# Input projections of u and v by seven half-size products instead of eight

## The reference

```python
h = rms_norm(x, g_mix[l])
z = h @ w_in[l]                       # 512 x 1024 by 1024 x 4800
u, v, q_lat, kv_lat, k_rope, gate_a, gate_b = jnp.split(z, offs, axis=-1)
y_a = spatial_gating(gelu(u), gelu(v), ...)      # layer norm of gelu(v), mixing of rows, times gelu(u)
y_b = mla_attention(q_lat, kv_lat, k_rope, ...)
merged = sigmoid(gate_a) * y_a + sigmoid(gate_b) * y_b
x = x + merged @ w_o[l]
x = x + moe(rms_norm(x, g_ffn[l]), ...)          # 64 experts, top 8
x = x + sigmoid(rms_norm(x, g_ple_in[l]) @ w_ple_gate[l]) * rms_norm(p[l] @ w_ple_proj[l], g_ple_out[l])
```

## Time and profile before

| | us |
|---|---|
| median of 3 runs (1110.62 to 1113.02) | 1111.32 |
| the profiled execution, whole | 1110.49 |
| its span in the trace | 1108.7 |
| TensorE busy | 1092.9 (99% of the span) |
| VectorE, ScalarE, GpSimd busy | 861.2, 787.0, 423.6 |
| chunks 2 to 9, by TensorE | 44.7 to 219.0 |

### The profile page before, as it was taken

One profiled execution on the slowest core, in us unless ns is written; L12 is line 12 of the kernel. 1 busy time (PEld: TensorE's weight loads), 2 busy tenths in 40 slices (PEclk: granted clock), 3 DMA queues, 4 the chain that ended last, 5 costly groups with the idle time before them and its releaser, 6 DMA issues.

```text
span 1108.7 us, 17836 instructions
## 1 busy us (share of the span) xinstructions
PE 1092.9 (99%) x5488; PEld 914.7 (83%) x5488; DVE 861.2 (78%) x1239; ACT 787.0 (71%) x1270; POOL 423.6 (38%) x477
## 2 busy tenths in 40 slices
PE   7999999999999999999999999999999999999998
PEld 7988888878778888888888888888888888888787
DVE  4535532278765468999999999999999999999865
ACT  6644433357654343888888898889888988888772
POOL 1120000015276003355556555555655555555400
PEclk9999999999999999999999999999999999999999
DMA  7422422112402259999999999999999999999632
GB/s 251 153 76 76 142 85 76 29 57 71 158 1 71 101 225 381 356 377 382 394 393 388 391 393 388 391 391 393 395 396 396 396 394 393 392 393 359 192 151 76
DMA packets 72130, 291.60 MB, mean 263 GB/s; under 512 B 15187, under 2 KB 20598, under 8 KB 47126
## 3 DMA queue, kind: packets, MB, share of 16 engines
q1 hardware_dynamic: 52672, 254.13, 57.3%
q0 software_dynamic: 18768, 34.79, 12.5%
q10 hardware_dynamic: 646, 2.12, 0.5%
HBM read 284.61 MB, written 42.07 MB: 295 GB/s over the span
## 4 chain that ended last, share of the span: by engine, by line
PE 93%; DVE 3%; ACT 2%; POOL 1%; issue 1%; DMA 0%; ACTq 0%; POOLq 0%; DVEq 0%
PE bank L2065 11%; PE bank L2067 11%; PE bank L2066 11%; PE bank L1752 7%; PE bank L1789 6%; PE bank L1793 6%; PE bank L1790 6%; PE bank L2093 5%; PE bank L2091 5%; PE bank L2092 5%; PE bank L2030 5%; PE bank L1743 2%; PE bank L1944 1%; PE bank L2163 1%; PE bank L2165 1%; PE bank L2164 1%
## 5 line engine op out<-in xcount | busy, mean ns | idle before, releaser
L1624 DVE TENSOR_TENSOR arena_r<-arena,win_r 128x1024 fp32r<-128x1024 f32 x252 | 292.0, 1221 | 21.9 <-ACT win_r L1082 19.1
L1082 ACT ACTIVATE win_r<-arena 128x1024 fp32r<-128x1024 f32 x252 | 246.5, 1069 | 0.5 <-DMA resid<-in_w_exp_up 0.5
L2065 PE MATMUL bank<-win_r,work_r 128*128 128x512 f32 x512 | 206.5, 403 | 0.6 <-issue 0.6
L2066 PE MATMUL bank<-win_r,x_low_r 128*128 128x512 f32 x512 | 199.5, 390 | 0.0
L2067 PE MATMUL bank<-arena_r,work_r 128*128 128x512 f32 x504 | 197.4, 392 | 0.0
L1604 DVE TENSOR_TENSOR arena_r<-arena,hT_r 128x1024 fp32r<-128x1024 f32 x128 | 150.5, 1217 | 0.5 <-ACT hT_r L1090 0.5
L733 POOL DMA_INDIRECT moe_sum<-ya,sidx x64 | 111.5, 1743 | 102.7 <-ACT ya L1118 86.0
L1789 PE MATMUL bank<-arena_r,hT_r 128*128 128x512 f32 (+2 forms) x320 | 121.9, 381 | 2.2 <-DVE win_r L1222 2.1
L1790 PE MATMUL bank<-arena_r 128*128 128x512 f32 (+2 forms) x320 | 121.1, 378 | 0.0
L1793 PE MATMUL bank<-win_r,hT_r 128*128 128x512 f32 (+2 forms) x320 | 121.0, 378 | 0.0
L2067 PEld LDWEIGHTS bank<-arena_r,work_r 128*128 128x128 f32 x504 | 94.6, 188 | 21.7
(11 more groups left out here) (321 smaller groups left out, 2213.4 us busy)
## 6 DMA issues: line engine op xcount, KB each, us to landing
arena<-in_w_exp_down SPq DMA_DIRECT2D x64, 1024.0 KB
arena<-in_w_exp_gate SPq DMA_DIRECT2D x63, 1024.0 KB
arena<-in_w_exp_up SPq DMA_DIRECT2D x63, 1024.0 KB
win<-in_w_in SPq DMA_DIRECT2D x8, 2048.0 KB, 7.8
win<-in_w_o SPq DMA_DIRECT2D x2, 2048.0 KB, 7.9
arena<-in_w_ple_gate SPq DMA_DIRECT2D x2, 2048.0 KB, 13.7
arena<-moe_sum SPq DMA_DIRECT2D x7, 512.0 KB, 7.0
win<-in_mla_w_qb SPq DMA_DIRECT2D x4, 576.0 KB, 4.0
```

The lines of the kernel that those rows point to most:

```text
L1082: act.activation(gu_hi[n % 2][:, :, cols], raw[:, :, cols], ACT.Copy).then_inc(gu_hi_r, 1)
L1624: dve.tensor_tensor(low_[:, :, cols], raw[:, :, cols], gu_hi[n % 2][:, :, cols].bitcast(F32), ALU.subtract).then_inc(gu_lo_r, 1)
L2065: pe.matmul(b_, x_hi[:, k, :], w_hi, start=(k == 0), stop=False)
L2066: pe.matmul(b_, x_lo[:, k, :], w_hi, start=False, stop=False)
```

## The change

Chunks 2 to 5 (v and u) are replaced by two **pairs** `p` = 0 (v) and 1 (u). In a pair the rows (512), the inner dimension (1024) and the columns (1024) are each cut in two, and the product is made with seven products of halves in place of eight (Strassen's method in Winograd's form). One product is 2 row tiles by 4 slices by 3 matmuls of 128x512, and they run in the order `11, T1, T2, 21, 22, T3, T4`. Four products take sums of rows (`S1` to `S4`), four take sums of weight quarters (`T1` to `T4`).

- **Rows.** VectorE makes S1 to S4 from `hT_hi` and `hT_lo` (`rows_1` to `rows_4`), once for both pairs; they are split in high and low parts. `rows_1` stands ahead of the split of chunk 1, the others behind it.
- **Weights.** The sums are made by DMA: SyncE loads a quarter, and GpSimd issues a DMA that adds another quarter on top (`add_weights`, `accum_op=ADD`). `T2` adds to what `T1` left, once VectorE has made `T1`'s low part; `T4` adds to `T2`. `T1(1)` below is T1 of pair 1. Each quarter is 128 x 4 x 512 values, 1 MB. Landings are counted on two semaphores.
- **Results.** `add_products` combines PSUM banks and SBUF on VectorE (14 instructions of 128x512 per pair), ScalarE copies the first product out and applies gelu in SBUF.
- **Gain.** `g_mix` goes to the transposed rows instead of the weights: `hT_evac` and `h_evac` become four 128x128 instructions per group; the splits become plain copies and subtractions, two slices at a time from chunk 1 on.
- **Start.** The tiles are transposed in another order (`x_T(2)` and `x_T(3)` inside the second tile); squares and the root come behind more of ScalarE's work. The raw weights use the place of `x` (`resid`), so `x` is loaded again later (4 loads of 512 KB).
- **Moved.** Latent scaling, angles, layer norm of v and GpSimd's rotary tables come behind the pairs, beside chunks 6 to 9. The gains `lng`, `lnb` and chunk 6 are loaded when product 22 of pair 1 is done.

In `order` rows below a line number is that of the kernel shown.

The core of the diff:

```diff
+        PRODUCTS = ("11", "T1", "T2", "21", "22", "T3", "T4")
+        PRODUCT_ROW = {"T1": "S1", "T2": "S2", "22": "S4", "T3": "S3"}
+        PRODUCT_BANK = {"11": 0, "T1": 4, "T2": 2, "21": 6, "22": 0, "T3": 4, "T4": 6}
...
+            def pairs_loads():
+                sp.wait_ge(tr_done, 2 * NT)
+                sp.wait_ge(rms_sq, NT)
+                half_load(v2(xr_, 0, HK, 512), half_chunk(0, "11"), ld_w0[0], 32)
+                half_load(v2(xr_, 2 * D, HK, 512), half_chunk(1, "11"), ld_w0[0], 48)
+                free(0)
+                half_load(v2(win0, 0, HK, 512), half_chunk(0, "22"), win_ready[0], 32)
+                half_load(v2(win0, 2 * D, HK, 512), half_chunk(0, "21"), win_ready[1], 32)
+                free(1)
+                half_load(v2(win1, 0, HK, 512), half_chunk(1, "12"), ld_w0[1], 48)
+                half_load(v2(win1, 2 * D, HK, 512), half_chunk(1, "22"), win_ready[1], 48)
...
+                sp.wait_ge(pj_done, products_done(NP - 1, "22"))
                 sp.dma_start(lng, bc(a["sgu_ln_g"][0], D)).then_inc(ld_ln, 16)
                 sp.dma_start(lnb, bc(a["sgu_ln_b"][0], D)).then_inc(ld_ln, 16)
...
+            def add_weights(p, name):
+                done, n = landed(p, name)
+                if n > 16:
+                    pool.wait_ge(done, n - 16)
...
+                pool.dma_start(dst, half_chunk(p, {"T1": "12", "T2": "22", "T3": "22", "T4": "21"}[name]),
+                               accum_op=ALU.add).then_inc(done, 16)
...
+            hT_evac(0, (0,))
+            split(0, range(2))
+            hT_evac(0, (1,))
+            split(0, range(2, KD))
             hT_evac(1)
-            for t in range(NT - 1):
-                square(t)
+            square(0)
+            square(1)
             hT_evac(2)
-            square(NT - 1)
+            square(2)
+            hT_evac(3)
+            square(3)
             act.wait_ge(rms_ms, NT)
             act.activation(st[2], st[1], ACT.Sqrt).then_inc(rms_rt, NT)
-            hT_evac(3)
...
+            high_part(0, "11")
+            high_part(0, "S1")
+            evac(1, 0)
+            high_part(0, "S2")
+            high_part(0, "T1")
+            evac(1, 1)
+            high_part(0, "S3")
+            high_part(0, "S4")
+            evac(1, 2)
+            evac(1, 3)
+            act.wait_ge(whi_used, 2 * KD)
+            high_part(0, "T2")
+            high_part(0, "21")
+            first_product_out(0)
...
+            rows_1()
             split(1)
+            rows_2()
+            low_part(0, "11")
+            low_part(0, "S1")
+            low_part(0, "T1")
+            rows_3()
+            rows_4()
+            low_part(0, "S2")
...
+                    for k in range(HK):
+                        if i == 0 and k % 2 == 0:
+                            pe.wait_ge(lo_ready, split_count(LOWS, p, name, k // 2))
...
+                        pe.matmul(b_, a_hi, w_hi, start=(k == 0), stop=False)
+                        pe.matmul(b_, a_lo, w_hi, start=False, stop=False)
+                        last = pe.matmul(b_, a_hi, w_lo, start=False, stop=(k == HK - 1))
+                last.then_inc(pj_done, 2 if name == "T4" else 1)
+            for p in range(NP):
+                for name in PRODUCTS:
+                    product(p, name)
```

More of the change, by code:

```diff
@@ L139, in hybrid_block_kernel @@
         sigb = v2(arena, o_sigb, NT, D)
-        hst = [arena[:, o_sigb + i * D:o_sigb + (i + 1) * D] for i in range(4)]
+        hst = [arena[:, o_qT + i * D:o_qT + (i + 1) * D] for i in range(4)]
         qrT = v2(arena, o_qrT, H // 2, SEQ)
@@ new lines, in h_evac, with row_hi, row_lo, lower_lo @@
+                    last.then_inc(tr_free[T % 2], 1)
+            first, second, upper, lower = slice(0, HT), slice(HT, SEQ), slice(0, HK), slice(HK, KD)
+            S1, S2, S3, S4 = (s_raw[n] for n in ("S1", "S2", "S3", "S4"))
+            def row_hi(ks, q):
+                return hT_hi[:, ks, q].bitcast(F32)
+            def row_lo(k_first, q):
+                return [z[:, :, q].bitcast(F32) for k0, _, z in hT_lo if k0 == k_first][0]
+            def lower_lo(z, q, op):
+                link(dve.tensor_tensor(z[:, 0:2, :], z[:, 0:2, :], row_lo(4, q), op))
+                return dve.tensor_tensor(z[:, 2:4, :], z[:, 2:4, :], row_lo(6, q), op)
@@ new lines, in rows_1, with rows_2 @@
+            def rows_1():
+                for i in range(2):
+                    dve.wait_ge(tr_free[i], NT)
+                link(dve.tensor_tensor(S1, row_hi(lower, second), row_hi(upper, second), ALU.subtract))
+                link(lower_lo(S1, second, ALU.add))
+                dve.tensor_tensor(S1, S1, row_lo(0, second), ALU.subtract).then_inc(combined, 1)
+            def rows_2():
+                dve.wait_ge(combined, 1)
+                link(dve.tensor_tensor(S2, S1, row_lo(0, first), ALU.add))
+                dve.tensor_tensor(S2, S2, row_hi(upper, first), ALU.add).then_inc(combined, 1)
@@ new lines, in low_part @@
+            def low_part(p, name, room=None):
+                if room is not None:
+                    dve.wait_ge(pj_done, room)
+                if name[0] == "S":
+                    dve.wait_ge(hi_ready, split_count(HIGHS, p, name))
+                    dve.tensor_tensor(s_lo[name], s_raw[name], s_hi[name].bitcast(F32), ALU.subtract).then_inc(lo_ready, 1)
+                    return
+                for part in range(2):
+                    dve.wait_ge(hi_ready, split_count(HIGHS, p, name, part))
+                    dve.tensor_tensor(B_LO[p][name][part][1], B_RAW[p][name][part][0], B_HI[p][name][part][1].bitcast(F32),
+                                      ALU.subtract).then_inc(lo_ready, 1)
@@ new lines, in split @@
+            def split(w, ks=range(KD)):
+                n, step = chunk_width(w), 1 if w == 0 else 2
+                for k in ks[::step]:
+                    z = slice(k, k + step)
+                    dve.wait_ge(hi_ready, KD * w + k + step + (4 - 2 * NP if w >= FIRST else 0))
+                    dve.tensor_tensor(v2(win_r[w % 2], 0, KD, n)[:, z, :], v2(win[w % 2], 0, KD, n)[:, z, :],
+                                      whi_r[:, z, 0:n].bitcast(F32), ALU.subtract).then_inc(lo_ready, step)
```

437 lines of the change are left out of this document (355 added, 82 removed).

## The result

| | before | after |
|---|---|---|
| median, us (4 runs each) | 1112.17 (1110.62 to 1113.42) | 1120.34 (1119.57 to 1121.28) |
| profiled execution, whole / span | 1110.49 / 1108.7 | 1121.28 / 1119.3 |
| first matmul of chunk 1 | 30.66 | 32.48 |
| stage of u, v and gates begins / ends | 44.7 / 219.0 | 46.6 / 230.0 |

The change makes the kernel **slower**: the ratio of the times is 1.0075, 95% interval 1.0057 to 1.0092, 8.2 us between the medians. The forecast was 1107.3 with a range up to 1114, so both the sign and the range were wrong.

The account below looks back on a forecast made before the run. The prediction took TensorE as the bound, busy 1092.9 of 1108.7 us. Its terms, -10.9 + 0.7 + 4.0 + 2.2 = -4.0 us, gave 1106.5 for the profiled execution and 1107.3 as median, range 1102.1 to 1114.0.

Parts of the forecast that it names:

- the pairs' junction: Between pair 0 and pair 1: forecast as free, with 1.8 us of slack at product T2; without it 1 to 2 us lost.
- Moved work: Work moved beside chunks 6 to 9: forecast to cost 0; without cover for a slower VectorE split, up to 2 us.
- Product T2: Pair 0: TensorE waits for T2's DMA-made weight sum; 4 us lost at 3.3 us per quarter, bounds 0 and 10.
- the turn: Loss at T2 in pair 0 that makes the change slower: from 8.0 us, about 4.5 us per quarter.
- The line under it: Trace row of q0, the queue with gathers and adding scatters: 11.83 MB in 23.0% of 200 us, 257 GB/s.
- The loss of about 1 us: T2 in pair 0, by the skill page's formula: 4.4 us for 1 MB, without sharing or a price for adding.
- The rival of slow sums: T2 in pair 0: 5.6 us per quarter plus slow GpSimd issues, T2 loses 15 us, 1118.3; chance 0.16.
- GpSimd kept from issuing: Ahead of T2: GpSimd issues only in gaps of VectorE's two-input subtractions; T2 loses 12 us, 1115.3; chance 0.05.
- The argument against this rival: Gathers in the expert stage, with VectorE busy 78% of the time, take 1057 to 1059 ns each.
- Chunk 6: Start of chunk 6: its load lands 0 to 1 us before the pairs' end; 2.2 us lost, bounds 1 and 3.5.
- The start: Start of chunk 1: first low part at 31.3 instead of 30.66; 0.7 us lost, from 0.3 gained to 2.0 lost.
- −10.9: The two pairs: 48 matmuls spared on TensorE at 0.227 us each, 10.9 us gained.

## Why the prediction was wrong, point by point

**Right.** TensorE was the bound and its matmuls keep their pace (0.23 us apart). No wait worth the name at the pairs' junction or inside pair 1; VectorE and ScalarE carry the products' work. Moved work behind chunk 6 costs nothing: chunks 6 to 9 have no idle time at all. The place of the largest wait, and its chain (VectorE behind ScalarE behind a DMA to `resid`), were as written; so was that it decides the sign.

**Product T2, 4.0 us forecast, 13.4 measured: the step that failed.** The price of an adding quarter was taken as 3.3 us, between 2.6 and 5.6. Measured is 5.1, and the upper bound was nearly right. The choice did not fit the working either: its two ends are 10 us of loss for 3.0 us of price, and a straight line between them gives 2.4 us lost at 3.3, 8.3 at 5.1, and the turn at 5.0 and not at 4.5. The reason given for the lower end was that the stretch with scatters and loads still moves 389 GB/s. That is a mean over 200 us, in which q0 carried 11.83 of 77.84 MB; it says nothing of how fast q0's part went. The line under it did: 23.0% of the engines' time for 15% of the bytes. The objection that many of its packets are small was a guess: the quarters, without small packets, cost nearly the 5.6 all the same.

**A later start and a fifth plain quarter were left out.** At 5.1 us per quarter that line has T2(0) landed at 62.4; it landed at 68.6. Two things account for most of the 6.2. The first sum was issued at 31.86, where the working has the quarter under it landed at 29.5: 2.4 us. And the working counts four plain MB beside the four adding ones; the queues carried five. From GpSimd's first issue to the landing of T2(0) (packets, MB, share of the engines):

```profile
q0 software_dynamic: 2199, 4.37, 66.0%
q1 hardware_dynamic: 2640, 5.24, 41.0%
```

The fifth is the quarter under T1(1), which SyncE issues at 31.2, just ahead of T1(0): 2.6 us. Four adding MB at 5.1 and five plain at 2.6 are 33.4 us of the 36.8 from issue to landing; the start of T3(1)'s sum, 0.18 MB, is another 0.9. Some 2.5 us are left for the time from issue to first byte and from last byte to release. It was paid about once: when T3(0) had landed and T1(1) was issued, plain loads kept the engines full (407 GB/s from 54 to 56 us, and a share of 1.05 up to 58). The Trainium skill, "DMA: Bandwidth & Descriptors", section "Anatomy of one DMA — SWDGE (gpsimd) path", has 2.0 us plus bytes over 436 GB/s; two such plain MB in one queue would be an estimate of 6.8 us by it, where the run with plain copies shows 8.0 and the run with adding 10.5. The loss of about 1 us that the prediction draws from the same formula does not come out of it: even four sums of 4.4 us one after another, with 1.6 for each issue, end at 53.5 from 29.5, and the low part at 55.8 is in time for 56.3.

**The rival of slow sums was the case that came true**, for one of its two reasons. It gave 15 us for T2 and 1118.3. Its price per quarter holds (5.1 for 5.6); its other part, 4.2 us for each issue on GpSimd, does not: the issues took 1.25 to 1.92. That its 15 us came near 13.4 is in part luck: the 5 us for slow issues stood where the late start and the fifth quarter were. It had 0.16, and by the two rows of q0 alone it deserved most of the weight. *GpSimd kept from issuing* is out: T4(0) was issued at 72.63 in 1.25 us, while VectorE ran L1481 twice, each time with two SBUF inputs, and the issue at 93.37, with VectorE idle beside it, took 1.27. The lock that the Trainium skill, "SBUF — State Buffer", section "SBUF: two separate sides", states for a VectorE instruction with two SBUF inputs is one against a GpSimd instruction that reads SBUF; for the issue of a DMA none shows in these rows. The argument against this rival was stronger than it was put: 78% is VectorE's share of the whole span, and beside those gathers it was busy for 57.9 of 60 us.

**Chunk 6, 2.2 forecast, 3.1 measured.** The terms were right: 10.3 for the load (10.4), and three issues of 0.4 (0.9 us to the last of the three). Their sum is 11.5 us against 10.9 to the pairs' end, so the load lands 0.6 *after* the end, not 0 to 1 before, and 0.6 + 1.07 + 1.22 = 2.9. This was a slip in adding up one's own numbers.

**The start, 0.7 forecast, 1.8 measured.** The reciprocal ran at 27.35 for 26.4, S1 from 27.46 to 31.4 for 26.5 to 30.5, the first low part from 31.51, and TensorE at 32.48 for 31.3. The chain was right and its head 1 us late; 0.4 of that is there from the first product on (its first matmul at 8.75 for 8.36), 0.25 of it since the first rows were transposed later (4.54 for 4.29). The order that stood in the diff was needed for nothing: the run with the start mended has no wait there.

**The clock was in no term.** After the waits of 13.4 and 3.1 us TensorE ran at 1.2 GHz for 13 steps, some 3.5 us by the windows. In the rows of before TensorE's longest wait for VectorE is 2.1 us, and the clock stands at full; but behind that wait, near the start, the trace of before has matmuls of 384 columns 0.32 us apart until 12.7 us, and 0.17 to 0.18 apart later:

```profile
8.36 0.66 PE L1789 MATMUL bank<-arena_r,hT_r 128*128 128x384 f32 x1 [2.10 <-DVE win_r L1222]
8.81 0.52 PE L1790 MATMUL bank<-arena_r 128*128 128x384 f32 x1
9.13 0.52 PE L1793 MATMUL bank<-win_r,hT_r 128*128 128x384 f32 x1
```

The clock's column reads 1.00 there, so it is open whether this is the same thing, but it was a reason to ask for a price after every wait that is forecast. That price is no fixed one: after waits of about 3 us ahead of chunk 6 the changed kernel has seven half-rate steps, the plain copies and the other order none; after waits of 2.4, 5.6, 5.9, 8.1 and 12.3 us ahead of T2 there are 7, 8, 8, 5 and 10, after that of 13.4 there are 6. What decides it these traces do not show.

By these measures the sum is −10.9 + 1.8 + 13.4 + 3.1 + 3.5 = +10.9 us, where the two profiled executions differ by 10.8. As the terms are read from the same windows, that they add up is no test of their causes; the experiments are.

## What to carry to other kernels

A sum made "for free" by an adding DMA takes twice the queue time of a load, and on a path that something waits for it must be priced by its own queue's share and bytes, never by the mean rate of a mixed stretch. Order DMAs by the time at which their data is needed, across queues too: here plain loads whose first split stands behind T2's shared the engines with the sum that TensorE waited for, and holding them back took 4 us off the wait and 6 off the time. Where a forecast holds a wait of TensorE, leave room for a low clock after it: up to 2.3 us here (ten half-rate steps after the wait of 12.3), and sometimes nothing. For a DMA that something waits for, follow the chain of DMAs that leads to it, and list every MB that any queue moves between the first issue and the last landing. One that was forgotten cost 2.6 us here.

## What the runs showed of the hardware that was not expected

- A DMA from GpSimd that adds into SBUF moved 197 to 209 GB/s with all 16 engines fully busy, a plain one from the same queue 393 in the window that it fills. Its instruction on GpSimd took 1.25 us or more, the plain one 0.75:

```profile
L733 POOL DMA_DIRECT2D resid<-in_w_in x6: 1255/1270/1582, 32.1 to 96.9; - x6
```

```profile
L733 POOL DMA_DIRECT2D resid<-in_w_in x6: 748/748/1007, 31.5 to 95.4; - x6
```

- A sum was slowed by what shared the engines with it: in the changed kernel T3(0)'s MB landed 21.9 us after its issue, with one more adding MB and plain loads beside it, where T1(0)'s took 10.5 with the plain loads held back.
- TensorE's granted clock fell to 0.50 within a wait of 13.4 us and came back about 3 us after work returned. It also fell after the wait of 3.1 us ahead of chunk 6 (0.83 and 0.75 in the two windows of 4 us there), but only once TensorE was at work again, and after waits of 3.1 and 3.2 us at the same place in two other kernels it did not. Nor did it in the kernels whose waits in this stage were 1.0 and 1.2 us.
